# Reordering the attention units of a two-layer hybrid encoder: groups A, D, B in place of D, A, B, with A's norm moved into the attention

## What is computed

```python
for l in range(DEPTH):                      # DEPTH = 2
    mod = ca @ w_ada[l] + b_ada[l]          # 12 units of 512 columns
    h = rms_norm(x, g_norm1[l]) * (1 + sc1) + sh1
    proj = h @ w_in[l]
    ya = diff_attention(...)                # group A: 4 heads, each two softmaxes, o = rms_norm(o, subln_g) * (1 - lam_init)
    yb = neighborhood_attention(...)        # group B: 4 heads, position bias
    yc = conformer_conv(...)                # group C: no attention
    yd = dilated_attention(...)             # group D: 4 heads
    x = x + gt1 * (concat([ya, yb, yc, yd]) @ w_out[l])
    h2 = rms_norm(x, g_norm2[l]) * (1 + sc2) + sh2
    x = x + gt2 * hier_moe(h2, ...)         # 32 experts, top 1 group, top 2 in it
return rms_norm(x, g_final)
```

## Time and profile before

| | |
|---|---|
| time, three runs | 1886.21, 1888.6 (median), 1890.51 us |
| the profiled execution's own time | 1887.05 us, span 1885.3 us |
| busy share of the span | PE 85%, DVE 33%, ACT 24%, POOL 11% |
| mean granted TensorE clock | 0.955 of full |
| attention, first layer | 211.3 to 340.2 us |
| attention, second layer | 1126.0 to 1255.1 us |
| output projection up to the router | 340.2 to about 412 us, and 1255.1 to about 1327 us |

### The profile page before, as it was taken

One profiled execution on the slowest core, in us unless ns is written; L12 is line 12 of the kernel. 1 busy time (PEld: TensorE's weight loads), 2 busy tenths in 40 slices (PEclk: granted clock), 3 DMA queues, 4 the chain that ended last, 5 costly groups with the idle time before them and its releaser, 6 DMA issues.

```text
span 1885.3 us, 22701 instructions
## 1 busy us (share of the span) xinstructions
PE 1602.5 (85%) x7556; PEld 774.6 (41%) x7556; DVE 623.1 (33%) x1337; ACT 453.5 (24%) x1007; POOL 209.3 (11%) x215
## 2 busy tenths in 40 slices
PE   5999888998988898887779998899699988878873
PEld 2455544553333333333235554454433333333331
DVE  1256366243222112222153825632421222221224
ACT  2110556321121111111121026651211111111111
POOL 2000022011111101011020002011111111111100
PEclk8999989998999999999989999999699999999997
DMA  9522344159999999999872325420799999999994
GB/s 353 171 90 89 140 149 154 56 198 395 374 398 407 415 403 408 412 410 417 342 260 90 111 70 174 161 83 23 257 384 362 402 413 407 410 416 409 404 408 172
DMA packets 119384, 527.57 MB, mean 280 GB/s; under 512 B 17040, under 2 KB 23280, under 8 KB 70416
## 3 DMA queue, kind: packets, MB, share of 16 engines
q1 hardware_dynamic: 101808, 493.66, 66.9%
q0 software_dynamic: 13104, 24.51, 4.2%
q10 hardware_dynamic: 4400, 8.46, 1.2%
HBM read 521.06 MB, written 23.86 MB: 289 GB/s over the span
## 4 chain that ended last, share of the span: by engine, by line
PE 60%; DMA 26%; DVE 6%; ACT 4%; issue 3%; SPq 1%; DVEq 0%; ACTq 0%; POOLq 0%
DMA ring<-in_w_exp_up 24%; PE ps L1257 21%; PE ps L938 17%; PE ps L1129 6%; PE ps L1255 3%; PE ps L1071 2%; PE ps L1085 2%; PE ps L1111 2%; PE ps L964 2%; DMA ring<-in_w_ada 1%; PE ps L1283 1%; PE ps L953 1%; DVE arena L642 1%; ACT arena L1545 1%; DMA arena<-yexp_d 1%
## 5 line engine op out<-in xcount | busy, mean ns | idle before, releaser
L1257 PE MATMUL ps<-ring,arena 128*64 128x512 f32 x2864 | 655.5, 610 | 122.9 <-ACT arena L1545 60.3
L1257 PEld LDWEIGHTS ps<-ring,arena 128*64 128x64 f32 x2864 | 220.9, 140 | 513.9 <-issue 503.0
L938 PE MATMUL ps<-ring,hT 128*128 128x512 f32 (+1 forms) x768 | 257.7, 493 | 5.1 <-ACT tmp L1440 4.9
L1539 ACT ACTIVATE arena<-ps 128x512 f32<-128x512 f32 x64 | 38.2, 597 | 806.7 <-PE ps L1257 753.2
L642 DVE TENSOR_TENSOR arena<-ps,arena 64x512 f32<-64x512 f32 (+1 forms) x64 | 44.4, 693 | 502.4 <-ACT arena L1539 434.3
L938 PEld LDWEIGHTS ps<-ring,hT 128*128 128x128 f32 x768 | 146.8, 194 | 104.2 <-issue 88.5
L903 POOL DMA_INDIRECT yexp_d<-arena,masks x64 | 59.3, 926 | 873.5 <-DVE arena L652 873.5
L650 DVE TENSOR_TENSOR arena<-ps,gate 64x512 f32<-64x512 f32 (+1 forms) x64 | 43.7, 683 | 278.9 <-PE ps L1257 258.4
L1129 PE MATMUL ps<-ring,hT 128*128 128x512 f32 x256 | 112.5, 595 | 0.0
L1531 ACT ACTIVATE arena<-ps,modc 128x128 f32<-128x128 f32 x256 | 96.2, 455 | 41.9 <-PE ps L1234 39.5
L1676 DVE SCALAR_TENSOR_TENSOR probsT<-z,convw,probsT 128x512 f32<-128x512 f32 x120 | 90.0, 751 | 3.9
(11 more groups left out here) (213 smaller groups left out, 1380.9 us busy)
## 6 DMA issues: line engine op xcount, KB each, us to landing
ring<-in_w_exp_down SPq DMA_DIRECT2D x128, 1024.0 KB, 23.7
ring<-in_w_exp_gate SPq DMA_DIRECT2D x124, 1024.0 KB, 21.2
ring<-in_w_exp_up SPq DMA_DIRECT2D x124, 1024.0 KB, 23.6
ring<-in_w_ada SPq DMA_DIRECT2D x24, 2048.0 KB, 8.6
ring<-in_w_in SPq DMA_DIRECT2D x8, 2048.0 KB, 23.1
ring<-in_w_out SPq DMA_DIRECT2D x4, 2048.0 KB, 8.1
ring<-in_w_in SPq DMA_DIRECT2D x6, 1024.0 KB, 11.1
xn_d<-arena ACTq DMA_DIRECT2D x8, 512.0 KB, 2.8
```

Source lines behind the costliest of these rows:

```text
L938: last = pe.matmul(out, lhs(k), rhs(k), start=(k == 0), stop=(k == n - 1))
L1257: last = [pe.matmul(outs[c][HALF * c:HALF * c + HALF, :], lhs(k)[:, 0:HALF], rhs(c, k), start=(k == 0), stop=(k == n - 1), tile_position=( ...
```

## The change

The attention units come in the order A, D, B. The order of the input projection stays D, A, B. A's norm moves to the steps 23 to 26: one average on PE at step 23 and one at step 24, both in bank 7; on ACT a logarithm and an exponential at step 24 and again at step 25; `subln` on DVE at step 26. A's features join the early part of the output projection, so that only B's are left for later. The third buffer pair for probabilities now lies in the rows that B's outputs will take, and D uses three pairs too. B's bias tables lie in the memory of A and then of D.

```diff
+ATTENTION = "ADB"
-UNITS = [(g, hp, t, h) for g in GROUPS for hp in range(2) for t in range(TT) for h in (range(2) if g == "A" else [None])]
+UNITS = [(g, hp, t, h) for g in ATTENTION for hp in range(2) for t in range(TT) for h in (range(2) if g == "A" else [None])]
-MEAN_STEP = NU + 1
+MEAN_STEP = 23
-K_EARLY, K_B, K_A = [4, 5, 6, 7], [2, 3], [0, 1]
-K_OUT = K_EARLY + K_B + K_A
+K_EARLY, K_B = [4, 5, 6, 7, 0, 1], [2, 3]
+K_OUT = K_EARLY + K_B
...
-            if step == MEAN_STEP:
-                for f in range(2):
-                    take((l, "meanA", f), (7, 3)[f])
+            if step - MEAN_STEP in range(2):
+                take((l, "meanA", step - MEAN_STEP), 7)
...
-        late_probs = v["D"].rearrange("p t c -> p (t c)").rearrange("p (f s) -> p f s", f=2)
+        late_probs = yT[:, FIRST_F["B"]:FIRST_F["B"] + 2, :]
-        bias_t = [qkT[g].rearrange("p f s -> p (f s)") for g in "DA"]
+        bias_t = [qkT[g].rearrange("p f s -> p (f s)") for g in "AD"]
...
-                    if i == MEAN_STEP:
-                        for f in range(2):
-                            mean_a(f)
-                        out_part(1, 0, K_EARLY)
-                    if i == MEAN_STEP + 1:
-                        out_part(1, 1, K_EARLY)
+                    if i - MEAN_STEP in range(2):
+                        mean_a(i - MEAN_STEP)
+                    if i > NU:
+                        out_part(1, i - NU - 1, K_EARLY)
...
+                    if i - MEAN_STEP - 1 in range(2):
+                        f = i - MEAN_STEP - 1
+                        key = (l, "meanA", f)
+                        await_filled(act, key)
+                        drains(act.activation(sqA[:, f, :], bank(key), ACT.Ln, bias=C["eps"]), key)
+                        await_drained(act, key)
+                        act.activation(sqA[:, f, :], sqA[:, f, :], ACT.Exp, scale=-0.5).then_inc(rootA_ready, 1)
...
-                    if i == NSTEP:
+                    if i == MEAN_STEP + 3:
                         subln()
```

More of the change, by code:

```diff
@@ L64 @@
 LAST_U = {g: max(u for u in range(NU) if UNITS[u][0] == g) for g in GROUPS}
-PAIR_OF = [2 * TT * GROUPS.index(g) + TT * hp + t for g, hp, t, h in UNITS]
+PAIR_OF = [2 * TT * ATTENTION.index(g) + TT * hp + t for g, hp, t, h in UNITS]
 NPAIR = PAIR_OF[-1] + 1
@@ L439, in unit_probs @@
         def unit_probs(u):
-            k = u % 2 if u < FIRST_U["A"] else (u - FIRST_U["A"]) % 3
+            k = u % 3 if u < FIRST_U["B"] else u % 2
             return (late_probs[:, 0, :], late_probs[:, 1, :]) if k == 2 else (prob[2 * k], prob[2 * k + 1])
@@ L446, in await_unit_probs @@
                 await_filled(eng, (l, "qkT", "B", TT - 1))
-            elif u == FIRST_U["A"] + 2:
-                await_filled(eng, (l, "o", PAIR_OF[LAST_U["D"]]))
+            elif u == 2:
+                await_filled(eng, (l, "v", "B", TT - 1))
             else:
-                old = u - 2 if u < FIRST_U["A"] + 2 else u - 3
+                old = u - 3 if u < FIRST_U["B"] + 2 else u - 2
                 await_filled(eng, (l, "probT", old, 0 if UNITS[old][0] == "A" else 1))
@@ L854, in _ @@
                 for hp in range(2):
-                    await_drained(pool, (l, "score", LAST_U["DA"[hp]], 1))
+                    await_drained(pool, (l, "score", LAST_U["AD"[hp]], 1))
                     for h in range(2):
@@ L1147, in _ @@
                         await_drained(pe, (l, "o", PAIR_OF[LAST_U["D"]]))
+                        pe.wait_ge(yA_ready, l + 1)
                         pe.wait_ge(conv_ready, 2 * (l + 1))
@@ L1170, in _ @@
                 await_drained(pe, (l, "o", NPAIR - 1))
[L1171 to L1174, removed]
                 pe.wait_ge(table_in, 16 * N_TABLES * (l + 1))
@@ L1178, in _ @@
                         for n in range(2):
-                            out_part(t, n, K_A if t < 2 else K_OUT)
+                            out_part(t, n, K_B if t < 2 else K_OUT)
                     if t == 0:
@@ L1497, in _ @@
                         ada_out(m, u, n % 2)
-                    if i == MEAN_STEP + 1:
-                        for f in range(2):
-                            key = (l, "meanA", f)
-                            await_filled(act, key)
-                            drains(act.activation(sqA[:, f, :], bank(key), ACT.Ln, bias=C["eps"]), key)
-                        for f in range(2):
-                            await_drained(act, (l, "meanA", f))
-                            act.activation(sqA[:, f, :], sqA[:, f, :], ACT.Exp, scale=-0.5).then_inc(rootA_ready, 1)
                 act.activation(spare[:, :], C["eps"], ACT.Sqrt)
```

## The result

The changed kernel took **1906.6 us** (median of four runs, 1904.95 to 1909.65) beside 1889.6 us for the kernel before on the same chip: ratio 1.0094, 95% interval 1.008 to 1.0109. The profiled execution has a span of 1905.0 us and a mean granted clock of 0.946. The forecast was 1896.6 us with a range up to 1905.0. So it is slower, as forecast, but by 17 us and not by 8, and outside the range.

What follows compares the result with a forecast made beforehand. PE was taken to bound the kernel, its attention time moving the end one for one. Terms summed to +4.0 per layer, +8 in all: 1887.05 to 1895, plus 1.55 for the median, 1896.6 us; range 1886.5 to 1905.

Steps and rivals of the forecast that it cites:

- (2): Attention start with A first: waits of 2.8 us against 2.4, so +0.4 per layer, bounds 0 and +1.7.
- (1): Seam D to A goes: 3.67 us of waits and 4.6 of half clock removed, -8.3 per layer.
- (3): A's steps with block transposes: two of four modulation units needing them move into D, -1.5 per layer, bounds 0 and -3.
- (4): Seam A to D: the 3.22 wait stays, new transposes wait behind DVE's maxima, +1.1 per layer, bounds 0 and 2.
- (5): Norm in steps 23 to 25: PE waits of 1.1, 3.3 and 3.3 us, +7.7 per layer, bounds 4 and 10.
- (6): Half clock behind the norm's waits in mid-attention: +4.6 per layer, bounds 0 and 8.
- (7): Tail: averages leave it for the middle (-1.98, +1.98), six early features instead of four; no change, 0.
- the clock holds: Rival: no half clock behind the norm's waits; 1887.4 (no difference, chance 0.10) or 1884 (faster, chance 0.12).
- the expert stream absorbs the difference: Rival: no effect at the end, the expert stream absorbs some microseconds; 1888.6, chance 0.08.
- The Trainium skill's drain: Rival: ACT table switches cost 1380 ns of drain besides the load, norm waits about 4.7 us; 1903, chance 0.05.
- the half clock lasts longer: Rival: half clock from step 24 into the projection, +8 in place of +4.6 per layer; 1903, chance 0.13.

Runs made afterwards that it cites:

- order_only: Kernel before with the order A, D, B alone; A's norm stays at the tail and four features stay early: 1881.0 us, ratio 0.9957.
- filled start: Changed kernel plus three unread 128x512 products in PE's wait behind the attention's first `ada`: 1898.0 us, ratio 1.0048.
- spread-out norm: Changed kernel with the second average at step 27 instead of 24 and `subln` at step 29: 1908.9 us, ratio 1.0114.
- without the tables: Changed kernel with exp(-mean) in place of A's logarithm, leaving out four table loads per attention: 1894.0 us, ratio 1.0024.

## Why the prediction was right in its sign and wrong in its size

**Term (2), "The start with A", is the step that failed.** The mechanism was named, and the size of its wait came out (2.71 and 2.70 for 2.8), but by luck: the forecast was 2.2 at the first turn's place and 0.6 for `mix` behind it. What came is 1.66 as before, 0.73 for the second exponential, and 0.31 because A's first scores take PE 1.60 us (210.32 to 211.92) where D's took 1.91; the waits for `mix` didn't show in this execution, where the slow clock covered them (0.40 in `order_only`, 1.45 with the start filled). The wait's consequence was wrong: "Bounds: 0 (the wait is today's) to +1.7 (the half clock follows, as for one seam below)". The half clock did follow, and cost 6.4 and 7.8, where the bound allowed 1.7. With the 0.3 of longer waits the term is +6.7 and +8.1, not +0.4: 14 us over both layers, more than the whole miss. The bound came from the seam A to B, where B's steps come behind a 3.22 wait. Behind the start come A's, and the one seam of before that A's steps follow, D to A, had 10 us of half clock, which the prediction had read and used for term (1). That row was the nearest one for (2) as well. The filled start bears it out: the same kernel without the long slow stretch there is 8.6 us faster, although a new wait of 1.45 takes some back. The size isn't steady, though: in layer 1 three like starts lost only some 2 us, so how much of the median's 17 us is this term is known no better than that 8.6.

**(1)** The seam D to A is gone, D and B follow each other without a wait over 0.3 us. As forecast, and by the sum its 8.3 per layer is why the order alone is faster. Filling the waits of the old seam, with A's steps still behind, won only 2.5 us of the 9 by its half clock: the gain needed the order, not only the waits gone.

**(3), (4)** Together -0.4 was forecast. PE's waits in A and at the seam behind it, without the 3.22, were 5.66 in layer 1 before (eight waits of 0.41 to 0.93) and are 5.03 now, the new one of 1.06 (1.1 forecast) among them: -0.6. The half clock behind the seam costs about 0.4 more (282.32 to 287.68 for work that took 4.94 at the seam A to B). About -0.2 in all, right in layer 1. In layer 2 the kernel before had one more slow stretch here, which the prediction did not read:

```profile
1212.73 0.23 PE L982 MATMUL ps<-tmp,cst 128*32 128x8 f32 x4 [0.75 <-DVE tmp L1651]
...
1213.37 1.92 PE L1111 MATMUL ps<-z,arena 128*64 128x128 f32 x16
```

A wait of 0.75, which layer 1 rode out at full clock (298.03), is followed by 3.4 us at half (1212.89 to 1216.27), 1.5 of PE time.

**(5)** 1.33 + 3.56 + 3.57 = 8.5 for 7.7, each released by what was named: `mod_out`, the logarithm, the logarithm. The two large ones were sized 0.26 short. The spread-out norm sharpens the reason: the wait is not one for a bank but for ACT's 3.9 us, which PE met in both placements at the next thing that it needed from ACT.

**(6)** 1.6 behind each of the two, 3.2 for 4.6. D's and B's steps follow, and the stretches are short. (5) and (6) together are 11.7 for 12.3; the difference to the order alone is 12.8 per layer by the times, 11.5 and 12.1 by the traces without the starts.

**(7)** Right: 29.40 of 29.40 us busy at full clock.

The measured terms add up to -8.3 + 6.7 + 0 + 8.5 + 3.2 = 10.1 in layer 1 and 11.5 in layer 2; the stretches grew by 9.0 and 10.1. The difference lies in small rows that no term had. In layer 1: -0.3 for A's first scores, -0.3 for a pause inside the old start's first turn (216.78 to 218.07 for 1.03 of work, at full clock), -0.2 for the wait of 0.20 at the old seam, -0.2 of (3) and (4), and -0.2 at a wait in B (0.30 for 0.46). In layer 2 it is the first three and the 1.5 us of before's extra slow stretch, less 0.9 that the seam A to D costs more there (1207.55).

**The rivals.** That the clock holds is refuted. That the expert stream absorbs the difference is refuted too: the attention's stretches grew by 19.0 us and the span by 19.7. The Trainium skill's drain ("ScalarE: Activation LUTs", "What ACT_TABLE_LOAD costs") doesn't show: a load in mid-stream starts 0.01 behind the accumulator read (308.19 and 308.20), and the logarithm 1.30 behind it, as with ACT idle before; without the tables each wait shrinks by 1.5 and not by the 2.7 of load and drain. That the half clock lasts longer was a rival, placed at step 24, and it lasted longer at step 2; that its 1903 lies nearest to the measured time is luck.

**What stays open** is what sets the length of a slow stretch. Shown is that a wait of 2.7 to 3.1 us was followed by 0 (narrow scores in D, both layers), 3.7 and 5.8 (D's steps), about 3 to 17 (A's steps) and 10 (A's steps with more work in them), one of 1.85 by 7 and 20 (A's steps with wide scores), and that the same program had a short and a long one in one execution. It goes with the steps behind the wait, but they don't settle it alone: layer 2 had the long one in all four kernels that start with A behind an unfilled wait of 2.7, layer 1 in one of them; which property of A's steps does it, their four transposes for eight, their missing attended pairs or their place, isn't shown, nor what differs between the layers. The narrow score products aren't it.

## What to carry to other kernels

Price a wait of the bounding engine by what it ran behind a like wait *with the same kind of work following*, and take a range, not one row: here waits of 2.7 to 3.1 us cost from nothing to 7.8 us on top of their own length, and from 2.0 to 7.8 with the same instructions following. When an engine is a shared server, moving its extra work, here 3.9 us on ACT, can merely move the place where others meet it; ask what is queued behind it on its own engine before spreading it. And judge a change of two parts by each alone: this one held a gain of 7 us and a loss of 26.

## What the runs showed of the hardware that was not expected

- Products that nobody reads pay. Three of 128x512 (2.84 us) in a wait of 2.7 took 8.6 us off the changed kernel and 7.7 off the order alone (1881.0 to 1873.3; some 10 by the ratios, 0.9957 to 0.9903), three more at the seam another 4.8.
- The engine that looks fully busy can be the one that loses most: 16.51 of 16.60 us busy at a clock of 0.59.
- The clock after a wait is not repeatable from layer to layer: 12.22 and 17.98 us for the same instructions behind the same 2.70. A wait of 0.75 was followed by nothing in one layer and by 3.4 us of half clock in the other, one of 1.45 by nothing in one layer of the filled start and by a stretch with a mean clock of 0.62 in the other.
- Two activations of 0.69 and 0.63 us from two tables hold ACT for 3.9 us (308.20 to 312.13), since a logarithm and the exponential right behind it each had a load of 1.28 of their own. The Trainium skill ("ScalarE: Activation LUTs", "Table sets: the hidden batching unit") would have one for both; the trace shows two every time.
